# A chain of two transformer blocks and a mixture of experts on one core: residual with tokens on partitions

## What is computed

```python
def modulated_sublayer(x, mod, g_pre, g_post, fn, weight):
    shift, scale, gate = mod[:, 0], mod[:, 1], mod[:, 2]
    h = rmsnorm(x, g_pre) * (1.0 + scale) + shift
    y = rmsnorm(fn(h), g_post)
    return x + weight * (1.0 + gate) * y
# first block: swiglu (d_ff 2816), pool mixer, swiglu; swiglu, latent attention (MLA), swiglu
# mod = silu(c) @ ada_w[i] + ada_b[i], nine rows of 1024 for each layer
# second block:
h = rms_norm(x, norm_mix);  x = x + hybrid_mixer(h, ...)   # conv, sparse attention, gated delta rule, w_out
h = rms_norm(x, norm_ffn);  x = x + hier_moe(h, ...)       # 32 experts of 512, 2 for each token
```

## Time and profile before

| | |
|---|---|
| time, median of 3 runs | 1891.42 us (1890.9 to 1893.22) |
| span of the profiled execution (page) | 1892.5 us; its own time is not listed apart from the three |
| PE busy | 1814.3 us, 96% |
| DVE, ACT busy | 969.8 us, 685.5 us |
| bytes read | 480.8 MB, mean 255 GB/s |
| chain of waits, shares | PE 43%, DMA 7%, DVE 3%, ACT 2%, issue 1% |

### The profile page before, as it was taken

How to read it: one execution, slowest core, us unless ns; L and a number is a source line. 1 busy time by engine, 2 the same in 40 slices (tenths; PEclk the granted TensorE clock), 3 DMA queues, 4 the chain that set the end, 5 groups by cost and what they waited for, 6 DMA issues and landing times.

```text
span 1892.5 us, 33006 instructions
## 1 busy us (share of the span) xinstructions
PE 1814.3 (96%) x13815; PEld 1487.2 (79%) x13815; DVE 969.8 (51%) x1398; ACT 685.5 (36%) x1052; POOL 21.3 (1%) x14
## 2 busy tenths in 40 slices
PE   7999989999999998999999999999999999999998
PEld 5999979999899986789998899988884554443434
DVE  3988668886875445455455786376621111111101
ACT  3444454444544425444444733456511111110101
POOL 0000000000000000000000112000000000000000
PEclk9999999999999999999999999999999999999999
DMA  9999619987484521254541332343359999999995
GB/s 392 424 372 341 235 68 351 347 337 267 176 322 173 194 90 67 101 195 173 192 174 68 134 134 101 131 181 125 134 228 377 425 426 424 425 425 426 424 426 214
DMA packets 45183, 483.48 MB, mean 255 GB/s; under 512 B 5008, under 2 KB 5136, under 8 KB 5904
## 3 DMA queue, kind: packets, MB, share of 16 engines
q1 hardware_dynamic: 44928, 480.79, 64.2%
q10 hardware_dynamic: 144, 1.05, 0.1%
HBM read 480.77 MB, written 1.05 MB: 255 GB/s over the span
## 4 chain that ended last, share of the span: by engine, by line
PE 43%; DMA 7%; DVE 3%; ACT 2%; issue 1%; DVEq 0%; SPq 0%; ACTq 0%
PE psG L436 24%; PE psA L436 9%; PE psS L436 9%; DMA mem<-stream 7%; DVE mem L2477 1%; PE psS L1377 0%; DVE parts L2162 0%; DVE mem L2730 0%; DVE mem L2246 0%; ACT mem L1590 0%; DVE st L2736 0%; PE psA L1034 0%; DVE mem L2475 0%; PE psS L1349 0%; DVE X L2255 0%
## 5 line engine op out<-in xcount | busy, mean ns | idle before, releaser
L436 PE MATMUL psG<-parts 128*128 128x256 f32 x6016 | 766.7, 286 | 11.7 <-DVE parts L2162 3.6
L436 PEld LDWEIGHTS psG<-parts 128*128 128x128 f32 x6016 | 739.7, 193 | 32.7 <-issue 19.2
L436 PE MATMUL psA<-parts 128*128 128x256 f32 x2368 | 303.2, 284 | 1.6 <-DVE parts L2335 1.6
L436 PEld LDWEIGHTS psA<-parts 128*128 128x128 f32 x2368 | 290.7, 192 | 17.7 <-issue 15.2
L2100 DVE TENSOR_TENSOR parts<-ring,parts 128x2048 fp32r<-128x2048 f32 x80 | 183.1, 2289 | 116.9 <-ACT parts L1555 116.8
L1555 ACT ACTIVATE parts<-ring 128x2048 fp32r<-128x2048 f32 x80 | 153.1, 1914 | 88.9 <-PE psA L436 88.5
L436 PE MATMUL psG<-mem 128*128 128x128 f32 (+4 forms) x1104 | 183.1, 430 | 1.8 <-DVE hparts L2758 1.1
L436 PEld LDWEIGHTS psG<-mem 128*64 128x64 f32 (+2 forms) x1104 | 98.4, 162 | 70.9 <-issue 65.6
L2091 DVE SCALAR_TENSOR_TENSOR mem<-ring,silc,mem 128x1536 f32<-128x1536 f32 (+1 forms) x98 | 138.8, 1417 | 2.5
L436 PE MATMUL psS<-ring,mem 128*64 128x512 f32 (+1 forms) x584 | 130.4, 593 | 3.0 <-issue 2.0
L436 PE MATMUL psS<-mem 128*64 128x512 f32 (+3 forms) x580 | 119.6, 531 | 13.2 <-DMA mem<-stream 12.4
(11 more groups left out here) (351 smaller groups left out, 1493.9 us busy)
## 6 DMA issues: line engine op xcount, KB each, us to landing
ring<-stream SPq DMA_DIRECT2D x223, 1536.0 KB, 8.2
mem<-stream SPq DMA_DIRECT2D x80, 1536.0 KB, 20.0
X<-x_in SPq DMA_DIRECT2D x1, 1024.0 KB, 17.7
ring<-stream SPq DMA_DIRECT2D x1, 1024.0 KB, 22.3
mem<-masks ACTq DMA_DIRECT2D x1, 1024.0 KB, 4.9
x_out<-X SPq DMA_DIRECT2D x4, 256.0 KB, 2.8
ring<-stream SPq DMA_DIRECT2D x1, 512.0 KB, 23.8
cst<-consts SPq DMA_DIRECT2D x1, 304.0 KB, 2.9
```

The costliest lines, as they stand in the source:

```text
L436: return nc.tensor.matmul(out, lhsT, rhs, start=start, stop=stop, skip_group_check=True)
```

## The change

X now has tokens on partitions: `X[P, TT, D]`, two tiles (TT) of 128 tokens by 1024 channels, loaded and stored in that form. Down, output and scatter products have the activations stationary (128 tokens) and 512 columns of the weights moving, into `psA[:, 2 * t + d, :]`. Norms are sums along the row, made by ACT's accumulator (`root_mean`). A passage is now: DVE multiplies y by the gate row (`gated`), ACT squares, sums, takes the root, DVE adds to X (`residual`), ACT the same for X, DVE scales X (`scaled`), PE turns it by 16 transposes into `psA` (`turn_x`), and ACT and DVE read it from there, with scale and shift, into high part, H and low part. It works in two halves of tokens, and the first half's y is signalled early (`y_half`). The gate row is spread over all partitions by eight matmuls with the identity (`gate_row`) and copied by ACT (`row_copy`). In ffn1 to ffn3 `first_two` replaces `first_gate_up` and the second `gate_up`. In the pool ACT makes the outcome and PE turns it (`token_major`, 16 transposes). The router needs no transposes of H, since the normed rows with the gain applied (`gain_d`, a new input of 0.5 MB, loaded on ACT's queue) serve the gather. ffn0 gets a `gate_row(0)` ahead of its last down product. The first norm goes the same way, its four copies of turned tiles by ACT ahead of the copy of the first modulation sums. The weights of w_o and w_out are packed by input channel instead of by output tile.

```diff
-        X = sb("X", [P, KT, S])
+        X = sb("X", [P, TT, D])
...
+        def norm_tok(n, t):
+            b = 0 if n < 6 else 18 if n == 6 else 16
+            return blk(b + t)
...
+            def gate_row(m):
+                pe.wait_ge(sem("mod_made"), 1 if m < 3 else 2 if m < 5 else 3)
+                if m:
+                    pe.wait_ge(sem("row_in"), m)
+                for k in range(KT):
+                    out = psA[:, 2 + k // 4, :] if m == 2 else psS[:, k // 4, :]
+                    last = mm(out[:, (k % 4) * P:(k % 4 + 1) * P],
+                              modC[:, m // 3, m % 3, k:k + 1].to_broadcast([P, P]), ident,
+                              start=(k % 4 == 0), stop=True)
+                last.then_inc(sem("row_sum"), 1)
...
+            def turn_x(n, t):
+                for q in range(2):
+                    pe.wait_ge(sem("xs_ready"), 4 * n + 2 * t + q + 1)
+                    for k in range(4):
+                        last = nc.tensor.transpose(turned_to(n, t, q)[:, k * P:(k + 1) * P],
+                                                   norm_tok(n, t)[:, (4 * q + k) * P:(4 * q + k + 1) * P], ident)
+                    last.then_inc(sem("turned"), 1)
+            def passage(n):
+                at = psA[:, 0, :] if n == 2 else None
+                idle(2, P, at)
+                if n < 6:
+                    gate_row(n)
+                pe.wait_ge(x_ready, 2 * n + 1)
+                idle(7, P, at)
+                pe.wait_ge(x_ready, 2 * n + 2)
+                idle(4, P, at)
+                turn_x(n, 0)
+                turn_x(n, 1)
+                idle(2, P)
+            def out_product(c, src, name):
+                for k in range(KT - 2):
+                    cc, a = c + k // 3, k % 3 * SLOT
+                    arrived(pe, cc)
+                    for t in range(TT):
+                        for d in range(2):
+                            last = mm(psA[:, 2 * t + d, :], src(k)[:, t * P:(t + 1) * P],
+                                      chunk(cc, a + d * 512, a + d * 512 + 512), start=(k == 0), stop=False)
+                    if k % 3 == 2:
+                        last.then_inc(chunk_used, 1)
+                arrived(pe, c + 2)
+                for t in range(TT):
+                    for k in (KT - 2, KT - 1):
+                        a = k % 3 * SLOT
+                        for d in range(2):
+                            last = mm(psA[:, 2 * t + d, :], src(k)[:, t * P:(t + 1) * P],
+                                      chunk(c + 2, a + d * 512, a + d * 512 + 512), start=False, stop=(k == KT - 1))
+                    if t == 0:
+                        last.then_inc(sem("y_half"), 1)
+                last.then_inc(sem(name), 1)
...
-                    for m in range(KT):
-                        for g, h in ((1, 0), (0, 1), (0, 0)):
-                            last = mm(psA[:, m // 2, (m % 2) * S:(m % 2 + 1) * S],
-                                      WD[t % 3][:, g, m * P:(m + 1) * P], AP[:, t % 2, h, :],
-                                      start=(first and m % 2 == 0 and g == 1), stop=final and g == h == 0)
+                    for tok in range(TT):
+                        for d in range(2):
+                            for g, h in ((1, 0), (0, 1), (0, 0)):
+                                last = mm(psA[:, 2 * tok + d, :], AP[:, t % 2, h, tok * P:(tok + 1) * P],
+                                          WD[t % 3][:, g, d * 512:(d + 1) * 512],
+                                          start=(first and g == 1), stop=final and g == h == 0)
+                        if final and tok == 0:
+                            last.then_inc(sem("y_half"), 1)
                     last.then_inc(sem("down_done"), 1)
...
+                def first_two():
+                    for f in range(2):
+                        pe.wait_ge(sem("hi_gu"), t0 + f + 1)
+                        pe.wait_ge(sem("act_ready"), t0 + f - 1)
                     for k in range(KT):
                         pe.wait_ge(sem("h_hi"), 8 * layer + k + 1)
-                        for u in range(2):
-                            term(u, 0, 0, k)
-                    if layer in AHEAD:
-                        pe.wait_ge(sem("lo_gu"), t0 + 1)
+                        for f in range(2):
+                            for u in range(2):
+                                term(f, u, 0, 0, k, u == 0 and k == 0, False)
+                    for f in range(2):
+                        pe.wait_ge(sem("lo_gu"), t0 + f + 1)
                         for u in range(2):
                             for k in range(KT):
-                                term(u, 1, 0, k)
+                                term(f, u, 1, 0, k, False, False)
+                    for f in range(2):
                         for k in range(KT):
                             pe.wait_ge(sem("h_lo"), 8 * layer + k + 1)
                             for u in range(2):
-                                last = term(u, 0, 1, k)
+                                last = term(f, u, 0, 1, k, False, k == KT - 1)
...
-                last.then_inc(sem("rt_htok"), 1)
-                idle(22, P)
+                idle(26, P)
...
-                    for m in range(KT):
-                        for h in (1, 0):
-                            last = mm(psA[:, m // 2, (m % 2) * S:(m % 2 + 1) * S], YS[:, h, m * P:(m + 1) * P],
-                                      SELT[:, p % 2, :], start=(first and m % 2 == 0 and h == 1),
-                                      stop=(final and h == 0))
-                        if final and m % 2 == 1:
-                            last.then_inc(sem("moe_acc"), 1)
+                    for t in range(TT):
+                        for d in range(2):
+                            for h in (1, 0):
+                                last = mm(psA[:, 2 * t + d, :], SELT[:, p % 2, t * P:(t + 1) * P],
+                                          YS[:, h, d * 512:(d + 1) * 512], start=(first and h == 1),
+                                          stop=(final and h == 0))
...
+            def root_mean(n, t, post):
+                src, out = (mixer_out(n, t), both(junk(n, t))) if post else (X[:, t, :], junk(n, t))
+                ch.link(A(out, src, ACT.Square, accum_out=sum_of(n, t, post)))
+                A(root_of(n, t, post), sum_of(n, t, post), ACT.Sqrt, bias=eps[:, 0:1], scale=1.0 / D)\
+                    .then_inc(sem("post_root" if post else "pre_root"), 1)
+            def pre_root(n, t):
+                ac.wait_ge(x_ready, 2 * n + t + 1)
+                root_mean(n, t, False)
+            def row_copy(m):
+                ac.wait_ge(sem("row_sum"), m + 1)
+                A(both(row_of(m)), psA[:, 2:4, :] if m == 2 else psS[:, :, :], ACT.Copy).then_inc(sem("row_in"), 1)
...
+            def passage(n, layer=None):
+                if n == 1:
+                    row_copy(0)
+                A(nst[:, 63:64], eps[:, 0:1], ACT.Sqrt)
+                if n < 7:
+                    for t in range(TT):
+                        ac.wait_ge(sem("y_gated"), 2 * (n - 1) + t + 1)
+                        root_mean(n - 1, t, True)
+                if n == 2:
+                    row_copy(n)
+                pre_root(n, 0)
+                if n in (1, 3, 4, 5):
+                    row_copy(n)
+                pre_root(n, 1)
+                if n == 7:
+                    for t in range(TT):
+                        ac.wait_ge(sem("turned"), 4 * n + 2 * t + 1)
+                        A(H[:, 0:4, t * P:(t + 1) * P], psA[:, t, :].rearrange("p (k s) -> p k s", k=4),
+                          ACT.Copy).then_inc(sem("h_ac"), 1)
+                    return
+                scale, shift = pre_cols(n)
+                for k in range(KT if n not in (1, 4) else 4):
+                    ac.wait_ge(sem("turned"), 4 * n + 3 + k // 4)
+                    if k == 4:
+                        ac.wait_ge(sem("h_step"), KT * NORMED[n] + 4)
+                    if n == 6:
+                        A(by_tok(HY[:, 0, k, :]), feature(k), ACT.Copy, scale=scale(k)).then_inc(sem("hy_hi"), 1)
+                    elif layer is not None:
+                        A(by_tok(HP[:, 0, k, :]), feature(k), ACT.Identity, bias=shift(k), scale=scale(k))\
+                            .then_inc(sem("h_hi"), 1)
+                    else:
+                        A(by_tok(H[:, k, :]), feature(k), ACT.Identity, bias=shift(k), scale=scale(k))\
+                            .then_inc(sem("h_ac"), 1)
+                if layer is not None and layer < 3:
...
+            def scaled(n, t):
+                ve.wait_ge(sem("pre_root"), 2 * n + t + 1)
+                r = root_of(n, t, False)
+                link(V.reciprocal(r, r))
+                if n == 7 and t == 0:
+                    ve.wait_ge(sem("gain_in"), 16)
+                for q in range(2):
+                    a = slice(q * 512, (q + 1) * 512)
+                    if n == 7:
```

(57 more changed lines are left out.)

657 lines of the change are left out of this document (263 added, 394 removed).

## The result

The changed kernel takes **1870.75 us** (median of 4 runs, 1870.06 to 1872.12) where the kernel before takes 1892.32 beside it: a ratio of 0.9876, interval 0.9856 to 0.9895. I had forecast 1846 and a range from 1830 to 1864. The sign is right, the size is half of what I forecast: 22 us instead of 45.

The account below looks back on a forecast made before the run. TensorE, busy 96%, was taken as the bound, with DMA the bound in the experts. Gains of 57.2 us less losses of 11.7 gave 45.5 net, from 1892.5 to 1847.0, stated as 1846 us; range 1830 to 1864.

Parts of the forecast that it names:

- The term of the down products: 88 FFN tiles: 12 matmuls of 512 columns at 218 ns replace 24 of 256 at 120, gaining 23.2 us.
- rival A: Down products: the 13 ns follow the columns, 512 take 240 ns, the 23.2 us vanish, 1869 us; chance 10%.
- The term of the FFN heads: Heads of ffn1 to ffn3: bare wait of 2.5 us before the first down product; net loss 1.7, 1.7 and 0.
- The clock: PE clock falling in or behind the new passages' waits: 5 us charged for all, bounds 0 and 18.
- the passages: Norms between stages, shortened by early token halves: 8.6 to 10.5 us after the FFNs and MLA, gaining 3.6 to 5.9 each.
- the router's matmuls: Before the router, token transposes go and X is added in halves: matmuls end at T + 7.5, not 11.1; gain 3.6 us.
- the gate row of ffn0: 16 records of 0.12 us on PE ahead of ffn0's last down product: loss of 1.9 us.
- rival C: DVE becomes the bound of the 42 tiles with modulation rows: 11 us stay, 1857 us; chance 6%.
- rival D: Down products: fp32r with 512 moving columns runs in two passes, 436 ns per matmul, 2077 us; chance 3%.
- the start: Four ACT copies ahead of the modulation sums' copy delay the first FFN matmul: loss 1.4 us, bounds 0 and 2.4.
- the scatter: Experts: 8 matmuls of 218 ns instead of 16 save 0.4 us per pair, mostly hidden behind DMA; gain 0.9 us.
- the hybrid's first slot: Passage into the hybrid, no gate row needed: first slot done at T + 16.5 instead of about 24.0; gain 7.1 us.

Follow-up runs that it names:

- experiments 10 and 11: The changed kernel with edits of experiment 4 and experiment 6, new start, passage fillers, earlier Silu load: 1853.12 us; with later gate row copy too: 1850.24 us.
- Experiment 5: The changed kernel with the head order of the kernel before in ffn1 to ffn3, tile 0 complete before tile 1: 1861.09 us, ratio 0.9827.
- experiment 7: The changed kernel with only filler matmuls added, before the first down products of ffn1 to ffn3 and in passages 2, 3 and 6: 1863.27 us, ratio 0.9836.
- experiment 6: The changed kernel with DVE splitting activations between the two products of the first modulation chunk, in every sixth tile with modulation rows: 1864.4 us, ratio 0.9842.
- experiment 4: The changed kernel with all low products of tile 0 ahead of tile 1's in the heads of ffn1 to ffn3: 1860.29 us, ratio 0.9821.

## Why the prediction was wrong

**The term of the down products failed: "I take 218".** It is 229, and the term is 11.4 us instead of 23.2. I took the row of w_out in plain f32 as the nearest, because a record of it lasts as long as 512 columns of streaming, and set aside the row of the right number format, because it had the wrong width. But the matmuls of w_out moved 256 columns, not 512: each of their two records took 218 ns, and with 512 columns a record takes 433. That row says nothing of 512 columns in fp32r, and neither does the experts' 214.5, which is plain f32 as well. The row of the right format does: it had 120 ns, 107 of them streaming. If the other 13 stay the same for each matmul, 512 columns take 213 + 13 = 227 ns; if they grow with the columns, 240 (rival A). The measured 229 lies by the first. My 218 left only 5 ns beside the streaming, which no fp32r row supports. By 227 the term would have been 14 us, near the 11.4 measured. The Trainium skill's formula for an isolated matmul (TensorE: Matmul & The Clock Gate, Back-to-back issue gap) gives 216 at 512 columns; the trace does not agree there either, 229.

**The term of the FFN heads failed in its size.** Mechanism and place were as forecast: the bare wait before the first down product in ffn1 and ffn2, behind DVE's modulation rows. I had 2.5 us; it was 3.82 and 2.46, and in ffn3 1.38 and then 0.67 where I had written 0. My step read the 4.4 us between the end of gate/up and the split from ffn2 of the kernel before and used it for ffn1 too, where the trace of before has 5.6 (290.82 - 5.76 = 285.06, and the split ends at 290.67). The difference is ACT's table load for Silu, 1.28 us, which stands behind tile 0's product in ffn1 and earlier in ffn2, in both kernels. It stands behind the product in ffn3 too (at 820.78 now), so that without it the two waits would be 2.5 us, as forecast, and 0.1. This is worked out from the rows; the load was moved only together with other edits (experiments 10 and 11). Experiment 5 shows what the old head would have been worth.

**The clock was a lump of 5 us.** Filler gave back 5.6 in the stretches where it stood (experiment 7). The hybrid's 1.6 stand beside that, unexplained by any edit: its 16 matmuls on 8 partitions took 4.8 us instead of 3.7 at a clock of 0.78, and the 48 behind them 8.0 instead of 7.5, with the same instructions. The bounds, 0 and 18, hold it; but I gave the clock no place. It fell where the waits were longest, in the FFN heads, which I had priced as waits alone, and in the passages into ffn1 and ffn2 (22 fillers in 4.28 and 4.14 us instead of 2.72). Heads and clock together cost 10.8 us in ffn1 to ffn3, against 3.4 for the heads forecast: (293.76 - 278.04) = 15.7 us from first gate/up to tile 2 before and 21.3 after in ffn1, 15.5 and 19.1 in ffn2, 15.5 and 17.2 in ffn3.

**Right:** the passages, 8.8 to 10.75 us where I had 8.6 to 10.5, by steps of ACT and DVE counted from shapes in other places; the router's matmuls, done 7.4 us after the output product (7.5 forecast); the gate row of ffn0, 1.7 us (1.9); DVE not the bound in tiles with modulation rows (rival C); one pass for 512 columns of fp32r (rival D). **Small misses:** the start, 2.4 instead of 1.4, of which about 1 us is the clock (with the same start the first product came 3.1 us sooner in experiments 5 and 6, so neither figure is firm); the scatter, 8 matmuls in 1.96 us, 245 ns each, so that nothing was won there; the pool, 0.8 instead of 1.6; the hybrid's first slot, done 18.1 us after T where I had 16.5; the experts, 0.8 lost where I had 0.9 gained, cause not looked for.

The sum of the misses: 11.8 (down products), 7.8 (heads with their clock, 11.2 with the down gain put back, less 3.4), 3.0 (passages, pool, router), 2.2 (start and ffn0's head), 1.6 (hybrid), 1.7 (experts), less 0.8 (MLA) and less the 5 us set aside for the clock: 22.3, against the 22.2 between the forecast span of 1847.0 and 1869.2.

## What to carry to other kernels

Price a matmul by the row with the same number format and work its width out from there, once with the part beyond streaming fixed and once with it growing, rather than by a row in another format that happens to last as long as you hope; and read from the shapes how many columns a row really moves. When two pieces of work are merged, ask what stood between the first one's end and its consumer: here 48 matmuls became 16, and putting one loop back was worth 10 us, half as much as the whole change had gained. When you carry a wait from one stage to another, go through every engine's steps in it: the table load in ffn1 could be read in the trace before. A wait of some microseconds on TensorE can cost twice, by itself and by the slow matmuls behind it; filler in the wait gave back the second part here at no cost, since it ended before the wait did. And a trace is one execution: before its total is put down to an edit, compare the stretches that the edit does not touch.

## What the runs showed of the hardware

- An fp32r matmul with 128 stationary columns took 120 ns for 256 moving columns and 229 for 512, whatever the bank order (229), the operand that stands still (120, tried at 256 columns) or a stationary operand of half the columns (230). Streaming is 107 and 213 ns of it; what the other 13 and 16 ns are stays open. The experts' scatter took 245 for 512, cause not looked for. In plain f32 each matmul stands as two records, of 218 ns for 256 columns (27.91 us for 128) and 433 for 512 (27.72 us for 64).
- Idle time of 3.8 us was followed by a whole product at 1.2 GHz (0.50 over 5.5 us), and in ffn2 2.5 us by 4.4 us for the 12 matmuls; waits of 1.7 and 1.9 us at the same place in ffn1 were not (2.8 us for the 12). After the same wait of 1.93 us in the passage into ffn1, the same 22 fillers took 4.28 us in the changed kernel, 4.35 in experiment 6 and 2.72 in experiments 4 and 5, whose passages are alike. The hybrid took 336.1 us in the changed kernel and 334.3 in experiment 4, with the same instructions. A stage can so differ by 1 to 2 us between kernels without any cause in its own instructions.
